# Seven products for eight in two more feed-forward blocks, the second layer's modulation on TensorE, and all sums of weights on VectorE

## The reference: what is computed

```
m = silu(cond) @ ada_w[l] + ada_b[l]          # 2 rows (latent, context) x 9 * 1024, per layer
h = rmsnorm(x, g_pre) * (1 + m[3j+1]) + m[3j]
x = x + weight * m[3j+2] * rmsnorm(block(h), g_post)

block of the feed-forward kind, D_FF = 2816:
    a, g = split(h @ w13)                     # 1024 -> 2 x 2816
    out  = (silu(g) * a) @ w2                 # 2816 -> 1024
```

## Time and profile before

| | |
|---|---|
| median of three runs | 2536.21 us (2535.64 to 2536.49) |
| the profiled execution | 2541.83 us, span 2540.0 us |
| TensorE matmul busy | 2476.5 us (97%) |
| VectorE, ScalarE, GpSimd busy | 1581.6 (62%), 764.9 (30%), 224.6 us (9%) |
| multiply-adds of the modulation on VectorE (L1848), both layers | 365.4 us |
| DMA: bytes, share of 16 engines | 278.64 MB, mean 110 GB/s; 36.4% |
| third block, from its first matmul to the next block's | 909.2 to 1382.8: 473.6 us |
| fourth block | 1382.8 to 1856.9: 474.1 us |
| sixth block, to the end of its last in-phase | 2093.1 to 2454.1: 361.0 us |

### The profile page before, as it was taken

How to read it: one execution, slowest core, us unless ns; L and a number is a source line. 1 busy time by engine, 2 the same in 40 slices (tenths; PEclk the granted TensorE clock), 3 DMA queues, 4 the chain that set the end, 5 groups by cost and what they waited for, 6 DMA issues and landing times. The chain is left out here.

```text
span 2540.0 us, 40285 instructions
## 1 busy us (share of the span) xinstructions
PE 2476.5 (97%) x15180; PEld 2295.7 (90%) x15180; DVE 1581.6 (62%) x2779; ACT 764.9 (30%) x1418; POOL 224.6 (9%) x299
## 2 busy tenths in 40 slices
PE   6999999999998899999999999999999999999998
PEld 5998999799888789989988998899799979989997
DVE  4887588734554678738875885233454458845864
ACT  4111111333444441111124211111331153523432
POOL 0000000201114210000002000000110011201211
PEclk9999999999999999999999999999999999999999
DMA  6554445333223335434551553222312223323332
GB/s 242 160 141 133 133 149 167 107 77 81 48 56 88 88 107 149 134 100 141 149 170 55 150 153 99 80 74 87 96 59 75 87 79 117 83 71 99 88 113 103
DMA packets 385035, 278.64 MB, mean 110 GB/s; under 512 B 39414, under 2 KB 354550, under 8 KB 383894
## 3 DMA queue, kind: packets, MB, share of 16 engines
q1 hardware_dynamic: 384918, 277.06, 36.4%
HBM read 270.04 MB, written 6.94 MB: 109 GB/s over the span
## 5 line engine op out<-in xcount | busy, mean ns | idle before, releaser
L1879 DVE TENSOR_TENSOR w_lo<-w_raw,w_hi 128x1024 fp32r<-128x1024 f32 (+1 forms) x363 | 354.5, 979 | 501.2 <-ACT w_hi L1303 496.8
L1303 ACT ACTIVATE w_hi<-w_raw 128x1024 fp32r<-128x1024 f32 (+1 forms) x363 | 309.2, 854 | 832.4 <-PE psum L921 425.3
L921 PE MATMUL psum<-hT_hi,w_hi 128*128 128x320 f32 x2432 | 554.8, 309 | 4.0 <-DVE w_lo L1879 3.3
L921 PE MATMUL psum<-hT_lo,w_hi 128*128 128x320 f32 x2432 | 554.1, 309 | 0.0
L921 PE MATMUL psum<-hT_hi,w_lo 128*128 128x320 f32 x2432 | 553.8, 309 | 0.0
L921 PEld LDWEIGHTS psum<-hT_hi,w_hi 128*128 128x128 f32 x2432 | 406.3, 188 | 5.7 <-DVE w_lo L1879 2.8
L921 PEld LDWEIGHTS psum<-hT_lo,w_hi 128*128 128x128 f32 x2432 | 406.8, 188 | 0.0
L921 PEld LDWEIGHTS psum<-hT_hi,w_lo 128*128 128x128 f32 x2432 | 406.6, 188 | 0.0
L1848 DVE SCALAR_TENSOR_TENSOR mod_acc<-ada_raw,cond_silu,mod_acc 128x256 f32<-128x256 f32 x896 | 365.4, 479 | 0.0
L848 PE MATMUL psum<-w_hi,act_hi 128*128 128x512 f32 x800 | 318.1, 398 | 4.6 <-DVE w_lo L1879 4.5
L849 PE MATMUL psum<-w_lo,act_hi 128*128 128x512 f32 x800 | 316.3, 395 | 0.0
(11 more groups left out here) (281 smaller groups left out, 3548.1 us busy)
## 6 DMA issues: line engine op xcount, KB each, us to landing
w_raw<-in_ffn_w_dram SPq DMA_DIRECT2D x156, 512.0 KB, 4.1
ada_raw<-in_ada_w_dram SPq DMA_DIRECT2D x128, 512.0 KB, 3.6
w_raw<-in_ffn_w_dram SPq DMA_DIRECT2D x148, 256.0 KB, 2.7
w_raw<-in_ab_w_in_dram SPq DMA_DIRECT2D x28, 512.0 KB, 4.1
w_raw<-in_sc_w_in_dram SPq DMA_DIRECT2D x24, 512.0 KB, 4.0
w_raw_next<-in_ffn_w_dram SPq DMA_DIRECT2D x20, 512.0 KB, 5.2
ada_first<-in_ada_w_dram SPq DMA_DIRECT2D x4, 2048.0 KB, 19.0
held_raw<-in_ffn_w_dram SPq DMA_DIRECT2D x28, 256.0 KB, 3.7
```

The costliest lines, as they stand in the source:

```text
L921: last = mm(IN[p][0:width, h, 0:HT], a, b[:, k, h * HT:(h + 1) * HT], start=(k == 0 and a is hi and b is hT_hi), stop=(k == KD - 1 and a i ...
L1303: A(dst, src, ACT.Copy).then_inc(w_hi_ok, 1)
L1879: V.tensor_tensor(d_, a, b.bitcast(F32), ALU.subtract).then_inc(w_lo_ok, 1)
```

## The change: what it does

- The third and fourth block get the scheme of the sixth: three plain pairs, then 8 and 11 pairs by seven products.
- The slices on VectorE for the second layer go. Nine blocks of 1024 columns of `ada_w[1]` are computed on TensorE inside the out-phases of these three blocks: three blocks in each first half and one in each second half of s = 2 and 3, and one in the first half of s = 5. A block is eight steps, one for each contraction tile; a step loads a tile of 128 x 1024 numbers (512 KB, three buffers in turn) and makes four matmuls of two-column weights and 256 columns in four 32-column groups of the array, all into one PSUM bank. `STEP_AT` says behind which unit of the out-phase a step stands. VectorE then adds the bias (4 small additions a block), and the rows go to DRAM.
- S1 and S2 move from GpSimd to VectorE for every pair.
- The PSUM banks of products and out-phases are dealt anew, so that one bank is free for the modulation; the waits of the out-phase's first unit change with it. `add_two` waits for the copy alone (`G_COPY`), no longer for one more step of ScalarE.
- The first pair of a second half is loaded only when the last modulation step of the first half has run, since they share a buffer.

```diff
-PLAIN = {5: (3, 0)}
+PLAIN = {2: (3, 0), 3: (3, 0), 5: (3, 0)}
...
-JOBS = {0: (0, 2 * D, (HF, HF), (3, 3)), 2: (1, 0, (HF, HF), (1, 1)), 3: (1, 6 * D, (HF, 0), (1, 0))}
+JOBS = {0: (0, 2 * D, (HF, HF), (3, 3))}
+MODS = {2: ([(1, 0), (1, D), (1, 2 * D)], [(1, 3 * D)]), 3: ([(1, 4 * D), (1, 5 * D), (1, 6 * D)], [(1, 7 * D)]), 5: ([(1, 8 * D)], [])}
+MW = 256
+STEP_AT = lambda half, n: [1 + j * 17 // 24 for j in range(8 * n)] if not half else [2 + j for j in range(8 * n)]
...
+        def out_bank(ph, d, t):
+
+            if ph.get("g1", 0) > ph.get("g0", 0):
+                return ((4, 5, 6, 7, 0), (2, 3, 4, 5, 6))[d][t] if ph["half"] == 0 else ((3, 4, 5, 6, 7), (1, 2, 3, 4, 5))[d][t]
+            return OUT[d][t]
...
-        G_COPY, G_ONE, G_TWO, G_HI = (lambda g, z=z: 4 * g + z + 1 for z in range(4))
+        G_COPY, G_ONE = (lambda g: 4 * g + (1 if g in BEGINS else 0)), (lambda g: 4 * g + 2)
+        G_TWO, G_HI = (lambda g: 4 * g + 3), (lambda g: 4 * g + (4 if g in ENDS else 5))
...
+            def load_bias_rows(ph, z):
+                b = ph["mb"] + z
+                layer, col = ph["mods"][z]
+                sp.wait_ge(mrow_ok, MROW(b - 1))
+                for i in range(4):
+                    dma(mod_bias[32 * i:32 * i + 2, :], bass.AP(ada_b.tensor, ada_b[layer, col + i * MW:].offset, [[0, 2], [1, MW]])).then_inc(bias_in, 16)
+
+            def load_mods(ph, u):
+
+                n = len(ph["mods"])
+                at_u = STEP_AT(ph["half"], n)
+                for j in range(8 * n):
+                    if max(2, at_u[j] + 3 - 2 * ph["half"]) != u:
+                        continue
+                    g = 8 * ph["mb"] + j
+                    if j == 0:
+                        load_bias_rows(ph, 0)
+                        sp.wait_ge(prod_lo_ok, SEVEN * ph["g1"])
+                    if j >= 3:
+                        sp.wait_ge(mod_mm, MM(g - 3))
+                    layer, col = ph["mods"][j // 8]
+                    slot, count = TILE(g)
+                    src = ada_w[layer].rearrange("(p k) n -> p k n", k=KD)[:, j % 8, col:col + 4 * MW].rearrange("p (a b) -> p a b", b=MW)
+                    dma(ada_tile[ph["half"]][slot][:], src).then_inc(ada_landed[slot], 16)
...
+                    if g == ph["g0"] and ph["half"] and ph["mb"]:
+                        sp.wait_ge(mod_mm, MM(8 * ph["mb"] - 1))
...
+            def modulation(ph, u):
+
+                n = len(ph["mods"])
+                bank = 0 if ph["half"] else 1
+                for j, at_u in enumerate(STEP_AT(ph["half"], n)):
+                    if at_u != u:
+                        continue
+                    g, k = 8 * ph["mb"] + j, j % 8
+                    if j == 0:
+                        pe.wait_ge(q_summed, U_CROSS(ph["g1"] - 1))
+                    elif k == 0:
+                        pe.wait_ge(mrow_ok, MROW(ph["mb"] + j // 8 - 1))
+                    slot, count = TILE(g)
+                    pe.wait_ge(ada_landed[slot], count)
+                    for i in range(4):
+                        last = mm(PS[32 * i:32 * i + 2, bank, 0:MW], csil[:, :, k], ada_tile[ph["half"]][slot][:, i, :], start=(k == 0), stop=(k == 7))
+                    last.then_inc(mod_mm, 1)
...
                         if seven(ph):
                             if t == 0:
                                 pe.wait_ge(q_summed, U_CROSS(ph["g1"] - 2))
                                 pe.wait_ge(q_gated, G_ONE(ph["g1"] - 2))
-                            if t == 2:
+                            if t == NT - 1:
                                 pe.wait_ge(q_gated, G_ONE(ph["g1"] - 1))
-                                pe.wait_ge(q_summed, U_TWO(ph["g1"] - 1))
-                            if t == NT - 1:
-                                pe.wait_ge(q_summed, U_CROSS(ph["g1"] - 1))
...
                     last.then_inc(pe_unit, 1)
+                    if seven(ph):
+                        modulation(ph, u)
...
-                        for g in range(ph["g0"] + 1, ph["g1"]):
-                            pool.wait_ge(pair_loaded[g % 2][0], 16 * (g // 2 + 1))
-                            pool.wait_ge(pair_loaded[g % 2][1], 16 * (g // 2 + 1))
-                            pool.wait_ge(prod_lo_ok, SEVEN * g - 1)
-                            pool.tensor_tensor(S1[:], A21(g), A22(g), ALU.add).then_inc(ws_ok, 1)
-                            pool.wait_ge(ws_ok, 4 * g + 1)
-                            pool.tensor_tensor(S2[:], S1[:], A11(g), ALU.subtract).then_inc(ws_ok, 1)
...
+            def modulation_rows(ph, z):
+
+                b = ph["mb"] + z
+                dve.wait_ge(mod_mm, MM(8 * b + 7))
+                dve.wait_ge(bias_in, BIAS(b))
+                dve.wait_ge(mod_stored, STORED(b - 1))
+                for i in range(4):
+                    rows = slice(32 * i, 32 * i + 2)
+                    V.tensor_tensor(mod_rows[ph["half"]][rows, :], PS[rows, 0 if ph["half"] else 1, 0:MW], mod_bias[rows, :], ALU.add).then_inc(mrow_ok, 1)
...
+                    if more:
+                        weight_sums(g + 1, 1)
                     if g > g0:
                         product(g - 1)
                         add_two(ph, g)
                     if more:
                         prod_rest(g + 1, 0)
+                        weight_sums(g + 1, 2)
```

More of the change, by code:

```diff
@@ L266, in build @@
         assert tail + 8192 + 4096 + HT * 4 <= end, end - tail
+        mod_bias = at("mod_bias", [P, MW], end // 32 * 32 - MW * 4)
+        assert held_at + 3 * 4096 <= end // 32 * 32 - MW * 4
+        mod_rows = [at("mod_rows0", [P, MW], end // 32 * 32 - 2 * MW * 4), at("mod_rows1", [P, MW], held_at - MW * 4)]
+        assert tail + 8192 + 4096 + HT * 4 <= end // 32 * 32 - 2 * MW * 4
+        ada_tile = [[at(f"ada_tile{h}{z}", [P, 4, MW], (tail if h == 0 else j0) + z * 4 * MW * 4) for z in range(3)] for h in range(2)]
+        assert 3 * 4 * MW * 4 <= 8192 + 4096 and j0 + 3 * 4 * MW * 4 <= held_at - MW * 4
         more_hi = at("w_hi_more", [P, 3, KH, P], where["gate"], F32R)
@@ L361, in build @@
         csil_ok, neg_ok = sem("csil_ok"), sem("neg_ok")
-        first_loaded = [sem(f"first_loaded{h}") for h in range(KD // 2)]
-        firstb_loaded, first_mm, first_row = (sem(n) for n in (
-            "firstb_loaded", "first_mm", "first_row"))
+        ada_landed = [sem(f"ada_landed{h}") for h in range(KD // 2)]
+        firstb_loaded, mod_mm, first_row = (sem(n) for n in (
+            "firstb_loaded", "mod_mm", "first_row"))
         ada_loaded = [sem("ada_loaded0"), sem("ada_loaded1")]
@@ L638, in load_in, with late_rows @@
                         load_job(ph, -1, i)
+            def late_rows(ph):
+                n = len(ph["mods"])
+                last = len(out_units(ph)) - 1
+                for z in range(n):
+                    if STEP_AT(ph["half"], n)[8 * z + 7] + 7 > last:
+                        store_mod_rows(ph, z)
+                        assert z == n - 1
             def load_pairs(s, w, ph, c0):
@@ L833, in _ @@
                     last = nc.tensor.transpose(PS[:, 7, col:col + 2], flat(mrow0[:])[:, kind * D + k:(kind + 1) * D:KD], ident[0:2, 0:2])
-            last.then_inc(first_mm, 1)
+            last.then_inc(mod_mm, 1)
             def sum_jobs(ph):
@@ L860, in turn_x @@
                             pe.wait_ge(mrow_ok, plan[s - 1][-1]["bt"] + 1)
+                    if t == 1 and plan[s - 1][-1].get("mods"):
+                        pe.wait_ge(mrow_ok, MROW(plan[s - 1][-1]["mods_end"] - 1))
                     if t in (1, 4):
@@ L940, in pair_products @@
                         pe.wait_ge(out_evac, ph["oe"] - NT + (1 if q else 0))
+                    elif new == 0 and q == 2 and ph["mb"]:
+                        pe.wait_ge(mrow_ok, MROW(ph["mb"] - 1))
                     elif new == 1 and q == 0:
@@ L1027, in out_phase @@
                             bank_free(d, t)
-                        last = weights(d, k, OUT[d][t], t, k == 0, k == K - 1)
+                        last = weights(d, k, out_bank(ph, d, t), t, k == 0, k == K - 1)
                         if k == K - 1 and t < NT - 1:
@@ L1050, in out_phase @@
                             turn_x(s + 1, t - 2)
-                        last = weights(1, k, OUT[1][t], t, z == 0, z == K - 1)
+                        last = weights(1, k, out_bank(ph, 1, t), t, z == 0, z == K - 1)
                         if t == NT - 1 and k in ring:
@@ L2034, in out_phase @@
                             split_held(s, ph, i)
+                    if seven(ph):
+                        for z in range(len(ph["mods"])):
+                            if min(STEP_AT(ph["half"], len(ph["mods"]))[8 * z + 7] + 4, len(units) - 1) == u:
+                                modulation_rows(ph, z)
                     z, r = divmod(u - 1 - LATE[ph["half"]] if late else u, 3)
-                    sooner = 2 if late and not final else 0
+                    sooner = 2 if (late or seven(ph)) and not final else 0
```

85 lines of the change are left out of this document (62 added, 23 removed).

## The result

| | before | after |
|---|---|---|
| median of the timed runs | 2536.49 us (7 runs) | 2547.63 us (2543.89 to 2553.89, 7 runs) |
| ratio to the kernel before | | 1.0041, 95% interval 1.0027 to 1.0055 |
| profiled execution, span | 2541.83, 2540.0 us | 2547.63, 2545.8 us |

The changed kernel is slower by 0.4%, 11.1 us by the medians. The profiled execution of after is at its median, that of before was 5 us above its own, so the two spans differ by only 5.8 us. The phases show where that comes from.

A forecast was written before the change was run, and what follows sets the result against it. TensorE's stream of matmuls was taken as the bound. -61.8 + 0.7 + 2.8 + 2.8 - 1.6 + 51.4 + 12.3 + 3.4 = +10.0 us on 2536.2 gave 2546 us; own range 2538 to 2558, 8 in 10 2519 to 2562.

The forecast's parts named there:

- In-phases (part 1): In-phases of the third and fourth block: seven products for eight shorten TensorE's stream, -61.8 us.
- Stalls of out-phases (part 1): Out-phases of third and fourth block: second unit's waits for VectorE +0.7 and +2.8, loads ahead of unit 2's weights +2.8 us.
- Sums (part 2): Pairs: two more sums on VectorE cost nothing, since it stays 2 us under TensorE's 12.3 us a pair.
- the rival in which VectorE becomes the bound: Pairs: `product` stays at 1.8 us, 0.5 us a pair over 57 pairs gives +28, 2574 us; chance 0.07.
- The stall let go (part 2): First half of the three blocks: `add_two` comes earlier, so a stall of 0.35 us and the like go, -1.6 us.
- The steps (part 3): Modulation on TensorE in out-phases: 72 steps at 0.43 us plus 55 interruptions at 0.37 us, +51.4, bounds 31 and 62.
- serial groups: Modulation steps: four column groups writing one PSUM bank don't run side by side, +93, 2639 us; chance 0.03.
- cheap places: Modulation steps in out-phases: 0.1 us an interruption, 5.5 us in all, as part of The cheap rival; chance 0.29.
- First tiles (part 4): Behind unit 1 of three first halves: TensorE loses 4.1 us each waiting for tiles, +12.3, bounds 6 and 18.
- The clock (part 5): Behind the first tiles' waits: half clock loses 1.7 us of work in two of three, +3.4, bounds 0 and 10.
- The cheap rival: Out-phases: 0.1 us an interruption, 2 us a first half for tiles, no clock drop, -14.6, 2521.6 us; chance 0.29.

The follow-up runs named there:

- doubled kernel: Changed kernel with every modulation step running its four matmuls twice, places, tiles and waits unchanged: 2571.17 us, ratio 1.0134.
- filled kernel: Changed kernel with 24 useless matmuls more in each first half, ahead of the wait for the first tile: 2539.08 us, ratio 1.0007.
- spaced kernel: Kernel with groups of three, its first-half groups spaced further apart, second halves back to single steps behind units 2 to 9: 2520.67 us, ratio 0.9929.
- groups of three: Late start with steps in groups of three, in 27 places for 51, and six tile buffers in a first half: 2531.57 us, ratio 0.9976.
- early tiles: Changed kernel with a first half's first two tiles issued behind unit 2's weights instead of unit 4's, ahead of the bias loads: 2532.78 us, ratio 0.9976.
- late start: Changed kernel with a first half's first steps behind unit 3 instead of unit 1, their tiles' queue place kept: 2532.98 us, ratio 0.9977.

## Why the prediction was right

It said 2546 us, and 2547.6 was measured. Step by step:

- **In-phases (part 1), -61.8.** Measured -60.8, and 135.6 us against 135.5 in the sixth block's shape. The missing 1 us is a stretch at half clock at the start of the third block, 148.1 for 147.2; the sixth block has one too, +1.1 in its first in-phase, where I had nothing.
- **Stalls of out-phases (part 1), 0.7 + 2.8 + 2.8.** The term was too large. TensorE's waits for `w_lo` in the out-phases rose from 6.7 to 8.6 us. Unit 1 of a second half waits 1.1 us, not 1.43, and the loads of the gate and the columns cost 0.2 us there, not 1.4. The out-phases grew by 69.9 us in all; with 48.1 for the steps, 11.8 for the first tiles and 8.5 for the clock, 1.5 is left for these stalls, where I had 6.3.
- **Sums (part 2), nothing.** Right, and shown by taking it back: 1.0040 against 1.0041. `product` at 818 ns and 2.25 us of VectorE idle a pair are as said, so the rival in which VectorE becomes the bound is out.
- **The stall let go (part 2), -1.6.** Wrong. The wait for `z_quarters` at the first pair is still there, 0.34 or 0.35 us in each of the three blocks:

```profile
976.26 0.38 PE L1053 MATMUL psum<-hT_hi,w_hi 128*128 128x320 f32 x1 [0.34 <-DVE z_quarters L2242]
```

- **The steps (part 3), 51.4.** 0.43 a step is right, in the rows and in the doubled kernel's second halves. The place was 0.31 for 0.37, so the term is 31.0 + 17.1 = 48.1, 3.3 us less. The rivals of serial groups and of cheap places fell by this.
- **First tiles (part 4), 12.3.** Measured 11.8: three waits of 3.7, 4.0 and 4.15 us. The issue was 0.9 us earlier than I had it, against unit 1's end, since a bias load costs 0.3 and not 0.5 us of the queue, and the landing took longer than 4.3 (the wait ends 5.1 us after the issue began). The estimate of 3.3 us a first half by the Trainium skill, "DMA: Bandwidth & Descriptors", section Anatomy of one DMA, is too small for this trace; that section gives its fit for loads that GpSimd issues, and ours go through SyncE's queue.
- **The clock (part 5), 3.4.** The term that was too small: three waits of three dropped the clock, two of them for 6.8 us. It is 8.5 us by the lengths of the stretches and 8.6 by the filled kernel.

Each cost that I named is there, and the direction follows from them. That the total is right to 2 us is luck: too much on stalls (5) and places (3), and too little on the clock (5) and the in-phases (4, with the stall of -1.6 that stayed), cancelled. The out-phases of first halves were told at 101 us and are 99.2 and 100.8. The sixth block came out 13.0 us longer to the end of its last in-phase, where I said some 10. "The third and fourth block come out about even": 472.1 and 472.8 us against 473.6 and 474.1.

The cheap rival, -14.6 us, was wrong of this kernel, but not far from what the same change does once its steps stand elsewhere: -18 us.

What stays open: I did not try why TensorE waits for VectorE at the border behind a second half once that half's stream is shortened. The rows show the wait (3.63, 2.51 us), not which piece of the chain ahead of it could be moved. The stretches at half clock at the start of a block are not explained either.

## What to carry to other kernels

Work put into a saturated engine's stream costs its own time, plus a fixed price at every place where it breaks the stream, plus whatever its first operand is late by; price the three apart, and look in the queue for where the first load stands. An idle wait of a few us on TensorE may cost nearly as much again in clock (here 11.8 us of waits and some 8.5 of clock), so a wait should be taken out by order (start later, or issue earlier) before anything else is tuned. When grouping gains nothing, look for the wait that took its place: the tiles of a group all arrive behind one another.

## What the runs showed of the hardware

- A change between full-width matmuls and two-column weights in four column groups, there and back, costs 0.31 us around one, two or three steps alike (rows at 1072.15 and 1076.39, and the windows of the spaced kernel).
- Four matmuls of two-column weights in four column groups, all into one PSUM bank, take 0.43 us together in all rows of one step. That is the pace at which four run side by side into a bank each at the kernel's start, for half the columns.
- Three loads of 512 KB in a row land 1.3 us apart, some 400 GB/s.
- In the changed kernel the clock fell from 2.4 to 1.2 GHz behind each of the idle waits of 3.7, 4.0 and 4.15 us, and did not fall where the same time was filled with 3.7 us of matmuls. With groups of three it fell behind 3.63 us at a block's border. Of shorter waits the runs show both: it fell behind 2.4, 2.9 and 2.7 us in the doubled kernel and 2.1 us in the early tiles' sixth block, and not behind 2.5 us in the late start's fourth.
- `product` on VectorE took 1812 ns with GpSimd's additions running beside it and 818 ns without them.
- Stretches at half clock at the start of a block (3.4 us) come and go between kernels whose blocks begin alike: at 905.6 and 2086.7 in after, in no block from the third on in before. With them one profiled execution differs from another by some us.
